# Attention on TensorE: values stationary, probabilities moving, even and odd heads on two column groups, and the division by the sum spread over partitions

## The reference, cut to what matters

```
z = rmsnorm_2(x, attn_norm) @ w_in          # pool channels, q, k, v, gates
a = pool_mixer(z[..., :1024], w_pool, pool_scale)
g_pool, g_attn = sigmoid(z[..., o4:] + b_gate)      # 2 x 1024 channels
# q: 16 heads of 64; k, v: 2 heads of 64, each shared by 8 q heads
s = einsum('bnqhgd,bnkhd->bhgnqk', q, k)    # blocks of 128 queries, keys of this block and the one before
m = maximum(max(s), sink);  p = exp(s - m)
denom = sum(p) + exp(sink - m)
b = einsum('bhgnqk,bnkhd->bnqhgd', p / denom, v)
x = x + (g_pool * a + g_attn * b) @ w_out
```

## Time and profile before

| | |
|---|---|
| time, median of 3 runs | 1514.95 us (1513.14 to 1514.98) |
| time of the profiled execution | 1514.69 us |
| its span in the trace | 1512.7 us |
| PE busy | 1420.0 us, 94% |
| DVE busy | 901.6 us, 60% |
| POOL busy | 836.7 us, 55% |
| ACT busy | 399.4 us, 26% |

### The profile page before, as it was taken

The page is one execution under the profiler, slowest core; times in us unless marked ns, Lnnn a source line. Parts: engine busy times, 40 slices in busy tenths (PEclk is TensorE's granted clock), DMA queues, the critical chain, the costliest instruction groups (busy, mean ns, idle before and its releaser), DMA issues.

```text
span 1512.7 us, 19663 instructions
## 1 busy us (share of the span) xinstructions
PE 1420.0 (94%) x6938; PEld 1148.8 (76%) x6938; DVE 901.6 (60%) x1256; ACT 399.4 (26%) x747; POOL 836.7 (55%) x651
## 2 busy tenths in 40 slices
PE   6799888999879999999998999799799999999998
PEld 3477667878658888888886887688688888888887
DVE  4469768775466666661008588634664888887000
ACT  2341221332242222221003202245422332332000
POOL 0224333442657666667775577333256777777765
PEclk9899999998989999999999999899899999999999
DMA  9437711211203333333332233111122333333332
GB/s 315 137 100 247 207 42 43 57 61 38 84 28 98 97 97 97 97 90 91 101 96 82 70 98 95 46 55 43 42 70 84 97 97 97 97 97 90 101 91 80
DMA packets 224314, 142.04 MB, mean 94 GB/s; under 512 B 5595, under 2 KB 210944, under 8 KB 224256
## 3 DMA queue, kind: packets, MB, share of 16 engines
q1 hardware_dynamic: 222389, 140.11, 31.3%
q10 hardware_dynamic: 1867, 1.12, 0.3%
HBM read 139.12 MB, written 2.10 MB: 93 GB/s over the span
## 4 chain that ended last, share of the span: by engine, by line
PE 79%; DVE 13%; ACT 3%; issue 2%; DMA 2%; POOL 1%; ACTq 0%; SPq 0%; DVEq 0%; POOLq 0%
PE ps L514 23%; PE ps L516 23%; PE ps L515 23%; DVE ada_acc L1635 2%; PE ps L554 2%; PE ps L1037 2%; DVE g_z L1736 1%; DVE norm_acc L1567 1%; PE ps L767 1%; PE ps L1007 1%; PE ps L1023 1%; DMA par_rows<-in_conv_w 1%; PE ps L595 1%; DVE SS L1818 1%; DVE xT L1986 1%
## 5 line engine op out<-in xcount | busy, mean ns | idle before, releaser
L477 POOL TENSOR_TENSOR w_lo<-raw,w_hi 128x1024 fp32r<-128x1024 f32 x213 | 535.9, 2516 | 17.8
L514 PE MATMUL ps<-h_hi,w_hi 128*128 128x512 f32 x1064 | 428.7, 403 | 16.2 <-DVE h_lo L1589 10.6
L516 PE MATMUL ps<-h_hi,w_lo 128*128 128x512 f32 x1064 | 420.7, 395 | 0.0
L515 PE MATMUL ps<-h_lo,w_hi 128*128 128x512 f32 x1064 | 420.4, 395 | 0.0
L473 POOL TENSOR_TENSOR w_hi<-raw,cst 128x16 fp32r<-128x16 f32 x213 | 65.1, 306 | 629.0 <-PE ps L516 563.5
L514 PEld LDWEIGHTS ps<-h_hi,w_hi 128*128 128x128 f32 x1064 | 203.7, 191 | 64.5 <-issue 17.2
L516 PEld LDWEIGHTS ps<-h_hi,w_lo 128*128 128x128 f32 x1064 | 203.3, 191 | 43.9
L515 PEld LDWEIGHTS ps<-h_lo,w_hi 128*128 128x128 f32 x1064 | 204.0, 192 | 40.1
L474 POOL TENSOR_SCALAR w_hi<-raw 128x1008 fp32r<-128x1008 f32 x213 | 229.9, 1079 | 0.0
L1907 DVE SCALAR_TENSOR_TENSOR f_acc<-ps,par,f_acc 128x441 f32<-128x441 f32 (+2 forms) x176 | 122.3, 695 | 48.9 <-ACT f_acc L1105 25.1
L514 PE MATMUL ps<-f_hi,w_hi 128*128 128x512 f32 x352 | 138.4, 393 | 0.2 <-POOL w_lo L477 0.2
(11 more groups left out here) (283 smaller groups left out, 2008.1 us busy)
## 6 DMA issues: line engine op xcount, KB each, us to landing
raw<-in_w_up SPq DMA_DIRECT2D x88, 512.0 KB, 3.9
raw<-in_w_in SPq DMA_DIRECT2D x59, 512.0 KB, 4.0
raw<-in_w_down SPq DMA_DIRECT2D x32, 512.0 KB, 3.8
v_tok<-in_w_ada SPq DMA_DIRECT2D x18, 512.0 KB, 6.1
ada_first<-in_w_ada SPq DMA_DIRECT2D x8, 1024.0 KB, 11.9
raw<-in_w_out SPq DMA_DIRECT2D x16, 512.0 KB, 3.8
ada<-in_w_ada SPq DMA_DIRECT2D x14, 512.0 KB, 5.7
raw<-in_w_down SPq DMA_DIRECT2D x16, 384.0 KB, 3.4
```

What stands on the lines that cost most here:

```text
L477: pool.tensor_tensor(w_lo[:, slot % 2, :], raw[:, slot, :], w_hi[:, slot % 2, :].bitcast(F32), ALU.subtract).then_inc(S("lo_split"), 1)
L514: nc.tensor.matmul(dst, lhs_hi, rhs_hi, start=first, stop=False)
L515: nc.tensor.matmul(dst, lhs_hi, rhs_lo, start=False, stop=False)
L516: return nc.tensor.matmul(dst, lhs_lo, rhs_hi, start=False, stop=last)
```

## The change

It does six things.

1. `weigh(s)` now holds 64 columns of `v2` stationary and moves `pt_sb`: for each half of the keys one matmul for the two even heads of the step and one for the two odd ones, 256 moving columns each. The even heads' result lands on PSUM partitions 0 to 63, the odd ones' on 64 to 127 (two column groups of the array), already with channels on partitions.
2. `turn_outputs`, `copy_outputs` and `o_tok` go. The reciprocal of the sum, which has tokens on partitions, is spread instead by `spread_shares(half)`: eight matmuls with one column of `att_stat`, repeated 64 times, as the stationary side and the identity (128 columns) as the moving side, odd and even heads again on the two column groups, into bank 5 (bank 1 for the last half). ACT copies it to `share` (`copy_shares`), DVE multiplies the weighed bank by it straight into `qT` (`outputs(half)`).
3. This is done for each half block (two steps, eight heads), eight times in all, no longer four times for a block; the sink's part and the reciprocal too (`shares(half)`).
4. `EARLY` is 7: gate tile 6 is computed before the pool mixing, and nine tiles, 27 parts, are laid into steps 0 to 13. ACT does `gate(2)`, `gate(3)`, `turned(6)`, `turned(7)`, `gate(4)` before `pool_hi(7)`, no longer behind it; DVE does `gate_scale(4)` before pool tile 7.
5. In a step ACT copies the turned probabilities before it takes a gate's tanh.
6. At the end DVE gates the first half of the last block, scales the second, splits two tiles, and then goes on; the output projection's results go to bank m in place of bank (m+7) % 8, and the up projection behind it waits for result 3 in place of 4.

```diff
-    EARLY = 6
+    EARLY = 7
...
+
+    def share_bank(half):
+
+        return 1 if half == 2 * BLOCKS - 1 else 5
...
         for s in range(2, EARLY):
             for part in range(3):
                 gate_part(s, part)
-            turn_heads(2 * s - 2)
-            turn_heads(2 * s - 1)
+            if s < 6:
+                turn_heads(2 * s - 2)
+                turn_heads(2 * s - 1)
...
                 pe.wait_ge(S("pt_copied"), 2 * s)
-            if n >= 1:
-                pe.wait_ge(S("bT_copied"), 2 * n)
             if s == 0:
                 pe.wait_ge(S("ya_ready"), 8)
             for i in range(4):
+                if i == 2 and s >= 2 and s % 2 == 0:
+                    pe.wait_ge(S("share_copied"), s // 2)
...
             if g % 2 == 0 and n >= 1:
-                pe.wait_ge(S("o_tok_ready"), 2 * (n - 1) + 1 + g // 2)
-            for i in range(4):
-                h = 4 * g + i
-                for half in halves(n):
-                    at = (i % 2) * 256 + half * P
-                    mm = nc.tensor.matmul(ps[:, 6 + h // 8, (h % 8) * HD:(h % 8 + 1) * HD], pt_sb[:, i // 2, at:at + P],
-                                          v2[:, n - 1 + half, (h // 8) * HD:(h // 8 + 1) * HD],
+                pe.wait_ge(S("o_scaled"), 2 * (n - 1) + 1 + g // 2)
+            at = (2 * g % 4) * P
+            for half in halves(n):
+                for odd in range(2):
+                    mm = nc.tensor.matmul(ps[odd * HD:(odd + 1) * HD, 6 + g // 2, at:at + 2 * P],
+                                          v2[:, n - 1 + half, (g // 2) * HD:(g // 2 + 1) * HD],
+                                          pt_sb[:, :, odd * 256 + half * P:odd * 256 + (half + 1) * P],
                                           start=(half == halves(n)[0]), stop=(half == 1))
             mm.then_inc(S("weighed"), 1)
 
-        def turn_outputs(n):
-            pe.wait_ge(S("o_tok_ready"), 2 * n + 2)
-            pe.wait_ge(S("pt_copied"), 8 * n + 8)
-            for k in range(KT):
-                mm = nc.tensor.transpose(ps[:, 4 + k // 4, (k % 4) * P:(k % 4 + 1) * P],
-                                         o_tok[:, k // 4, (k % 4) * P:(k % 4 + 1) * P], const("ident", P))
-                if k % 4 == 3:
-                    mm.then_inc(S("o_turned"), 1)
+        def spread_shares(half):
+
+            pe.wait_ge(S("share_ready"), half + 1)
+            if half == 2 * BLOCKS - 1:
+                pe.wait_ge(S("gate_scaled"), 16)
+            else:
+                pe.wait_ge(S("pt_copied"), 4 * half + 4)
+            stat = att_stat[:, half // 2 % 2, 4, :]
+            for k in range(4):
+                for odd in range(2):
+                    h = 8 * (half % 2) + 2 * k + odd
+                    mm = nc.tensor.matmul(ps[odd * HD:(odd + 1) * HD, share_bank(half), k * P:(k + 1) * P],
+                                          stat[:, h:h + 1].broadcast_to([P, HD]), const("ident", P), start=True, stop=True)
+            mm.then_inc(S("share_spread"), 1)
 
         STEPS = 4 * BLOCKS
         scores(0)
@@ -1054,25 +1065,24 @@
             parts = gate_parts(s)
             if parts:
                 gate_part(*parts[0])
-            if s and s % 4 == 0:
-                turn_outputs(s // 4 - 1)
+            if s and s % 2 == 0:
+                spread_shares(s // 2 - 1)
             if s + 1 < STEPS:
                 scores(s + 1)
             turn_probs(s)
+            if s == STEPS - 1:
+                spread_shares(2 * BLOCKS - 1)
             if len(parts) > 1:
                 gate_part(*parts[1])
             weigh(s)
-        turn_outputs(BLOCKS - 1)
-
-        pe.wait_ge(S("gate_scaled"), 16)
-        pe.wait_ge(S("bT_copied"), 2 * BLOCKS)
+
...
         for p in range(8):
+            if p == 7:
+                gate(2)
+                gate(3)
+                turned(6)
+                turned(7)
+                gate(4)
...
-        gate(2)
-        gate(3)
-        turned(6)
-        turned(7)
-        gate(4)
-        turned_and_gates(4)
+        turned(8)
+        turned(9)
+        gate(5)
+        gate(6)
...
-        def copy_outputs(n):
-            for i in range(2):
-                act.wait_ge(S("o_turned"), 2 * n + i + 1)
-                activate(qT[:, 4 * i:4 * i + 4, n * P:(n + 1) * P], ps[:, 4 + i, :].rearrange("p (k t) -> p k t", k=4), ACT.Copy)\
-                    .then_inc(S("bT_copied"), 1)
+        def copy_shares(half):
+
+            act.wait_ge(S("share_spread"), half + 1)
+            if half >= 2:
+                act.wait_ge(S("o_scaled"), half - 1)
+            activate(share[:, half % 2, :], ps[:, share_bank(half), :], ACT.Copy).then_inc(S("share_copied"), 1)
 
         for s in range(STEPS):
             probs(s)
+            if s and s % 2 == 0:
+                copy_shares(s // 2 - 1)
+            copy_probs(s)
+            if s == STEPS - 1:
+                copy_shares(2 * BLOCKS - 1)
             if s and gate_done_in(s - 1):
                 gate(gate_done_in(s - 1))
-            if s and s % 4 == 0:
-                copy_outputs(s // 4 - 1)
-            copy_probs(s)
-        copy_outputs(BLOCKS - 1)
         for k in range(KT):
             if k % 4 == 0:
                 act.wait_ge(S("y2_sum"), k // 4 + 1)
...
+            elif p == 7:
+                gate_scale(4)
...
-        for s in range(4, EARLY):
+        for s in range(5, EARLY):
             gate_scale(s)
...
-            if g == 3:
+            if g % 2:
                 dve.wait_ge(S("max_negated"), s + 1)
-                vec.tensor_tensor(stat[:, 3, :], sinks[:, :], stat[:, 1, :], ALU.add).then_inc(S("sink_offset"), 1)
-
-        def outputs(n):
-
-            stat = att_stat[:, n % 2]
-            dve.wait_ge(S("probs_ready"), 16 * n + 16)
-            dve.wait_ge(S("sink_part"), n + 1)
-            link(vec.tensor_tensor(stat[:, 2, :], stat[:, 2, :], stat[:, 3, :], ALU.add))
-            link(vec.reciprocal(stat[:, 4, :], stat[:, 2, :]))
-            if n >= 1:
-                dve.wait_ge(S("o_turned"), 2 * n)
-            for i in range(2):
-                dve.wait_ge(S("weighed"), 4 * n + 2 * i + 2)
-                vec.scalar_tensor_tensor(o_tok[:, i, :].rearrange("p (h e) -> p h e", e=HD),
-                                         ps[:, 6 + i, :].rearrange("p (h e) -> p h e", e=HD), 0.5,
-                                         stat[:, 4, 8 * i:8 * i + 8].unsqueeze(2).broadcast_to([P, 8, HD]),
-                                         ALU.mult, ALU.mult).then_inc(S("o_tok_ready"), 1)
+                hs = slice(4 * g - 4, 4 * g + 4)
+                vec.tensor_tensor(stat[:, 3, hs], sinks[:, hs], stat[:, 1, hs], ALU.add).then_inc(S("sink_offset"), 1)
+
+        def shares(half):
+
+            n, i = half // 2, half % 2
+            stat, hs = att_stat[:, n % 2], slice(8 * i, 8 * i + 8)
+            dve.wait_ge(S("probs_ready"), 8 * half + 8)
+            dve.wait_ge(S("sink_part"), half + 1)
+            link(vec.tensor_tensor(stat[:, 2, hs], stat[:, 2, hs], stat[:, 3, hs], ALU.add))
+            vec.reciprocal(stat[:, 4, hs], stat[:, 2, hs]).then_inc(S("share_ready"), 1)
+
+        def outputs(half):
+
+            n, i = half // 2, half % 2
+            dve.wait_ge(S("share_copied"), half + 1)
+            dve.wait_ge(S("weighed"), 2 * half + 2)
+            vec.scalar_tensor_tensor(qT[:, 4 * i:4 * i + 4, n * P:(n + 1) * P], ps[:, 6 + i, :].rearrange("p (k t) -> p k t", k=4), 0.5,
+                                     share[:, i, :].rearrange("p (k t) -> p k t", k=4), ALU.mult, ALU.mult).then_inc(S("o_scaled"), 1)
 
         def pool_gated(k):
...
-            if s and s % 4 == 0:
-                outputs(s // 4 - 1)
+            if s and s % 2 == 0:
+                shares(s // 2 - 1)
             if s + 1 < STEPS:
                 maxima(s + 1)
+            if s and s % 2 == 0:
+                outputs(s // 2 - 1)
...
-                    dve.wait_ge(S("bT_copied"), 2 * BLOCKS - 2)
+                    dve.wait_ge(S("o_scaled"), 2 * BLOCKS - 2)
...
-        outputs(BLOCKS - 1)
+        shares(2 * BLOCKS - 1)
         dve.wait_ge(S("gate_tanh"), 16)
         order.done(attention_gated(KT - 1, slice(0, T - P)))
-        for half in range(2):
-            dve.wait_ge(S("bT_copied"), 2 * BLOCKS - 1 + half)
+
+        def last_gated(half):
+
+            dve.wait_ge(S("o_scaled"), 2 * BLOCKS - 1 + half)
             attention_gated(slice(4 * half, 4 * half + 4), slice(T - P, T)).then_inc(S("y2_sum"), 1)
-        for k in range(KT):
+
+        def y2_low(k):
+
             dve.wait_ge(S("y2_hi_ready"), k + 1)
             vec.tensor_tensor(y2_lo[:, k, :], qT[:, k, :], y2_hi[:, k, :].bitcast(F32), ALU.subtract).then_inc(S("y2_ready"), 1)
 
+        last_gated(0)
+        outputs(2 * BLOCKS - 1)
+        y2_low(0)
+        y2_low(1)
+        last_gated(1)
+        for k in range(2, KT):
+            y2_low(k)
+
```

21 lines of the change are left out of this document (9 added, 12 removed).

## The result

The changed kernel took 1496.83 us (median of 4 runs, 1491.75 to 1501.94), the kernel before beside it 1514.05 us (median of 4, 1509.79 to 1514.98): a ratio of 0.9896, with a 95% interval of 0.9866 to 0.9926. It is faster. Its profiled execution took 1501.94 us, with a span of 1500.2 us against 1512.7 before, 12.5 us less.

What follows compares the result with a forecast made beforehand. PE's own work was taken to bound the steps, with a hole ahead of the pool mixing and the tail also slow. Terms A, B and C, -5.1 - 1.1 - 4.4 = -10.6 from 1514.69, gave 1504.1 us, range 1498 to 1511.

Steps and rivals of the forecast that it cites:

- Term A: Ahead of the attention: the hole before the pool mixing goes, though gate 6 moves in; -5.1 us.
- rival 4: Ahead of the pool mixing: weight units come late, so the gate tile does not fit the hole; 1509 us, chance 0.08.
- Term B: PE's work in the steps up to `scores(14)`: cheaper `weigh`, no `turn_outputs`, added `spread_shares`; -1.1 us.
- Term C: From `scores(14)` to the output projection: 24.0 us instead of 28.4, with a new wait at `spread_shares(6)`; -4.4 us.
- rival 5: Tail and projection: full clock returns ahead of the projection, whose 3.1 us half-clock loss goes; 1499 us, chance 0.13.
- 1: In `weigh` and `spread_shares`: the two column groups do not overlap; +17 us, 1521, chance 0.08.
- 2: In the steps: the shares' round trip stalls PE, one us in six steps; +6 us, 1510, chance 0.10.
- 3: At `weigh` and `spread_shares`: each full-array/half-array change empties the array; +9.6 us, 1514, no change, chance 0.05.

Runs made afterwards that it cites:

- hole alone: The kernel before with only the work ahead of the attention changed (`EARLY` 7 and its ScalarE and VectorE order), attention as before; ratio 0.9946.
- attention alone: The changed kernel with `EARLY` 6 and the old order ahead of the attention put back; ratio 0.9994.
- tanh first: The changed kernel with ScalarE doing the gate's tanh ahead of the copies again, as before the change; ratio 0.9929.
- groups in turn: The changed kernel with the even heads' two matmuls in `weigh` first, then the odd heads' two; ratio 0.9929.
- one column group: The changed kernel with `weigh` reordered, odd heads written over even heads on partitions 0 to 63, so even heads' outputs are left out; ratio 0.9989.
- step 0 filled: The changed kernel with three gate parts in step 0, two ahead of `turn_probs(0)`, and each later part half a step earlier; ratio 0.9910.

## Why the prediction was right, and where its sizes were off

The forecast was faster, and it is. The predicted 1504.1 us lie 2.2 above the profiled execution; the median, 1496.83, is 1.2 below the range's low end, and the ratio times the median of before gives 1499.2. The sum was -10.6 and the stages gave -12.3. No mechanism that it named failed; four sizes were off, and one effect, half clock behind the wait of step 0, had no term. That B still came near its size is luck: two errors of 0.9 and 1.5 us had opposite signs.

- **Term A** was put at -5.1; it is -5.6, and the run "hole alone" gives it without any new attention. From the key transposes to `scores(0)` PE took 17.3 us, not the 17.7 of the sum (the transposes 0.8 and not 1.0, and almost nothing at the changes), and they started 0.2 us earlier. Weights and the pool tile were in time, so rival 4 is out.
- **Term B** was put at -1.1 and is -0.5, but of two parts. The work itself gives -2.0, as "attention alone" shows. From the starts of the groups: all 13 `weigh` in the steps -7.1, `turn_outputs` -2.9, `spread_shares` +6.1, and +1.8 in the gate groups beside them: ahead of each of the 13 `weigh` the 0.09 of the earlier trace rows, the rest for the most part where `spread_shares` stands and behind the half-array groups. I had `weigh` at 1.16 with its entry and it is 1.10, and I had counted block 0 at nothing where it gives 0.23 less 0.09 each. The other part, +1.5, I missed: with the hole filled, the old wait of 2.0 us in step 0 is followed by half clock.
- **Term C** was put at -4.4 and is -5.2. The chain was right in its order and its first places: `spread_shares(6)` at a+9.1 (predicted a+9.3), a wait of 5.1 (5), released by the reciprocal. Then `scores(15)` came at a+11.0 (predicted 10.4 at full clock) and the projection 12.2 later (11.5). I had taken 2.0 us for half clock, of 4.3 at the worst, on top of a+22, and the tail ended at a+23.2. Half clock added 0.9 to `spread_shares(6)` and 0.9 to `scores(15)`, as their rows show; the start 0.2 earlier and a rest of the chain 0.4 shorter than summed took 0.6 off.
- **The projection** was left as it was and gave 1.0 more: half clock covers some 3.4 us of it (0.90 as a mean over 16.9 us), no longer its first 6.2. That is rival 5 in part. In "tanh first" and "groups in turn" the granted clock of the first 6.2 us is 1.00, with the same tail, so this number hangs on the single trace.

Of the rivals, 1 is refuted by "one column group", which shows what it would have cost. 2 is refuted by the waits: none at a share from step 1 to 13. 3 named a drain of up to 0.24 us more at each change of layout. The Trainium skill ("TensorEngine Tiling (Array Packing)", Key Properties) says that a change of tiling mode drains TensorE; the traces have 0.09 us ahead of such a group and 0.12 within it, 0.21 for in and out together, so if it drains, no more than that is the price here.

What the 12.3 us are made of: 5.6 are a repaired wait ahead of the attention. The steps give 0.5, which is 2.0 from the new attention's matmuls less 1.5 for half clock. The tail gives 5.2, of which 3.0 come with the hole alone and 2.1 only with both. The projection gives 1.0, within 0.8. What stays open is why half clock follows step 0's wait in all eight kernels that fill the hole and keep this wait, and not in the two that still have the hole. The wait is 2.0 us in all ten; "step 0 filled" shows that without it the drop does not come, but not what tells the two cases apart. Nor do the runs show why the projection starts at half clock in the changed kernel and not in two others with the same tail.
